# Attention softmax: ScalarE, not VectorE, multiplies the exponentials by the reciprocal sums, and TensorE asks for the weighted sample rows one step later

## What is computed

```
def cross_attend(h, k, v, w_q, w_o):
    q = einsum('btd,de->bte', h, w_q)                       # 4 heads of 256
    s = einsum('bthd,bmhd->bhtm', q, k) * 256 ** -0.5       # 256 memory rows
    p = softmax(s, axis=-1)
    o = einsum('bhtm,bmhd->bthd', p, v)
    return einsum('bte,ed->btd', o, w_o)
```

## Time and profile before

| what | value |
|---|---|
| median of 3 runs | 2838.85 us (2838.82 to 2842.92) |
| the profiled execution: its own time | 2840.13 us |
| its span, first to last instruction | 2838.4 us |
| granted TensorE clock, mean over the span | 0.939 |
| TensorE busy | 2506.3 us, 88% |
| VectorE busy | 1411.8 us, 50% |
| GpSimd busy | 1289.9 us, 45% |
| ScalarE busy | 430.7 us, 15% |

### The profile page before, as it was taken

How to read it: one execution, slowest core, us unless ns; L and a number is a source line. 1 busy time by engine, 2 the same in 40 slices (tenths; PEclk the granted TensorE clock), 3 DMA queues, 4 the chain that set the end, 5 groups by cost and what they waited for, 6 DMA issues and landing times. The chain is left out here.

```text
span 2838.4 us, 37980 instructions
## 1 busy us (share of the span) xinstructions
PE 2506.3 (88%) x14950; PEld 2403.9 (85%) x14950; DVE 1411.8 (50%) x1582; ACT 430.7 (15%) x728; POOL 1289.9 (45%) x842
## 2 busy tenths in 40 slices
PE   4967879777699689999799999999999997799996
PEld 4967879777699669888799999999999996698886
DVE  5999999999744452332622232322312234523324
ACT  3110110101111321122310000000000003211212
POOL 2734444434355454344544444444444445543452
PEclk7988999888899789999899999999999997999998
DMA  2111111111121132233011111111111111322331
GB/s 91 54 37 44 48 47 51 46 29 45 53 73 57 38 112 78 67 115 111 26 46 46 45 45 41 45 45 41 45 45 45 41 44 37 112 79 67 114 111 63
DMA packets 224013, 168.55 MB, mean 59 GB/s; under 512 B 10746, under 2 KB 219138, under 8 KB 223922
## 3 DMA queue, kind: packets, MB, share of 16 engines
q1 hardware_dynamic: 214002, 156.78, 18.0%
q10 hardware_dynamic: 9920, 10.48, 1.1%
HBM read 152.29 MB, written 14.93 MB: 59 GB/s over the span
## 5 line engine op out<-in xcount | busy, mean ns | idle before, releaser
L147 POOL TENSOR_TENSOR w_hi<-w_raw,ones 128x512 fp32r<-128x512 f32 x404 | 576.3, 1427 | 1407.4 <-PE PS L211 1225.5
L211 PE MATMUL PS<-h_hi,w_hi 128*128 128x364 f32 x2880 | 646.8, 333 | 61.0 <-DVE e_V L828 39.1
L150 POOL TENSOR_TENSOR w_lo<-w_raw,w_hi 128x512 fp32r<-128x512 f32 x404 | 644.1, 1594 | 31.7
L211 PE MATMUL PS<-h_hi,w_lo 128*128 128x364 f32 x2880 | 642.4, 332 | 0.0
L211 PE MATMUL PS<-h_lo,w_hi 128*128 128x364 f32 x2880 | 641.6, 331 | 0.0
L211 PEld LDWEIGHTS PS<-h_hi,w_hi 128*128 128x128 f32 x2880 | 502.8, 190 | 66.7 <-DVE e_V L828 40.3
L211 PEld LDWEIGHTS PS<-h_hi,w_lo 128*128 128x128 f32 x2880 | 506.6, 190 | 0.0
L211 PEld LDWEIGHTS PS<-h_lo,w_hi 128*128 128x128 f32 x2880 | 505.7, 190 | 0.0
L851 DVE SCALAR_TENSOR_TENSOR e_C<-e_V,prm,e_C 128x1024 f32<-128x1024 f32 x240 | 322.8, 1345 | 0.3
L211 PE MATMUL PS<-y_hi,w_hi 128*128 128x364 f32 x1152 | 261.6, 336 | 61.7 <-ACT e_GS L702 25.9
L211 PEld LDWEIGHTS PS<-y_hi,w_hi 128*128 128x128 f32 x1152 | 201.5, 192 | 69.5 <-issue 45.0
(11 more groups left out here) (194 smaller groups left out, 2164.0 us busy)
## 6 DMA issues: line engine op xcount, KB each, us to landing
w_raw<-in_w_in_odd SPq DMA_DIRECT2D x128, 256.0 KB, 2.8
w_raw<-in_w_in_even SPq DMA_DIRECT2D x80, 256.0 KB, 2.9
a_KV<-in_cache_mem_k SPq DMA_DIRECT2D x64, 256.0 KB, 4.9
a_KV<-in_cache_mem_v SPq DMA_DIRECT2D x64, 256.0 KB, 4.3
w_raw<-in_w_out_even SPq DMA_DIRECT2D x32, 256.0 KB, 2.7
w_raw<-in_w_k SPq DMA_DIRECT2D x32, 256.0 KB, 2.9
w_raw<-in_w_v SPq DMA_DIRECT2D x32, 256.0 KB, 2.8
w_raw<-in_w_q SPq DMA_DIRECT2D x32, 256.0 KB, 2.8
```

The lines of the kernel that those rows point to most:

```text
L147: c.nc.gpsimd.tensor_tensor(by_128(c.Wh[:, s, :]), by_128(c.Wraw[:, s % RAW, :]), ones, ALU.mult).then_inc(self.w_hi, 1)
L150: c.nc.gpsimd.tensor_tensor(c.Wl[:, s, :], c.Wraw[:, s % RAW, :], c.Wh[:, s, :].bitcast(F32), ALU.subtract).then_inc(self.w_split, 1)
L211: mm = pe.matmul(ps[:, q, 0:PART], w, a[:, q * PART:(q + 1) * PART], start=first and n == 0, stop=last and n == 2)
```

## The change

The multiplication of the prompt's `a_E` by the reciprocal of its sums moves from VectorE to ScalarE. There it is an activation `Copy` with a scale for each partition, behind `copy_turned` of the round. The two multiplications of the sample sets `a_ES` move too, to ScalarE's round 5. VectorE keeps the maxima and the reciprocals. TensorE waits for the sample sets (`s_weighed`) ahead of `turn_samples`, and no longer ahead of `turn(5)`.

```diff
@@ TensorE, round t
-                    if t == S_TURN:
-                        pe.wait_ge(s_weighed, h * SETS + SETS)
                     turn(h, t)
                     if t + 2 < NT:
                         scores(h, t + 2)
                     if t == S_TURN:
+                        pe.wait_ge(s_weighed, h * SETS + SETS)
                         turn_samples(h)
@@ ScalarE, round t
                     if t >= 1:
                         copy_turned(t - 1)
+                    act.wait_ge(inverted, h * NT + t + 1)
+                    s.activation(E[:, t % 2, :], E[:, t % 2, :], ACT.Copy, scale=SUM[:, t % 2:t % 2 + 1]).then_inc(weighed, 1)
+                    if t == S_TURN:
+                        act.wait_ge(s_inverted, h + 1)
+                        for m in range(SETS):
+                            s.activation(ES[:, m, :], ES[:, m, :], ACT.Copy, scale=SUMS[:, m:m + 1]).then_inc(s_weighed, 1)
                     if t == S_TURN + 1:
                         act.wait_ge(s_turned, h + 1)
@@ VectorE, round t
                     dve.wait_ge(exped, h * NT + t + 1)
                     v.reciprocal(SUM[:, i:i + 1], SUM[:, i:i + 1]).then_inc(inverted, 1)
-                    dve.wait_ge(inverted, h * NT + t + 1)
-                    v.tensor_scalar(E[:, i, :], E[:, i, :], SUM[:, i:i + 1], None, ALU.mult).then_inc(weighed, 1)
@@
                     if t == S_TURN - 1:
                         dve.wait_ge(s_exped, h * SETS + SETS)
                         v.reciprocal(SUMS, SUMS).then_inc(s_inverted, 1)
-                        dve.wait_ge(s_inverted, h + 1)
-                        for m in range(SETS):
-                            v.tensor_scalar(ES[:, m, :], ES[:, m, :], SUMS[:, m:m + 1], None, ALU.mult).then_inc(s_weighed, 1)
```

## The result

The changed kernel takes 2825.93 us (median of 6 runs, 2824.28 to 2831.71), the kernel before 2841.02 in its 6 runs on the same chips (2838.82 to 2844.67): 15.1 us less, a ratio of 0.995 with a 95% interval of 0.9937 to 0.9963. The profiled execution took 2825.71 us with a span of 2823.9, against 2840.13 and 2838.4.

A forecast was written before the change was run, and what follows sets the result against it. It took a ring of dependent TensorE and VectorE steps in the softmax part, filled by no engine, as the bound. -7.0 + 2.2 - 1.8 - 4.6 = -11.2 us against 2840.1 gave 2828.9, range 2824.5 to 2836.5.

The forecast's parts named there:

- VectorE is held by GpSimd's splits: Around round 5, heads 1 to 3: VectorE multiplications last until GpSimd's weight split ends, 1.23 us instead of 0.35.
- The price on ScalarE: Each moved 128x256 multiplication takes 0.51 us on ScalarE, bounds 0.47 and 0.64.
- A plain round grows by 0.20: Each ordinary softmax round: 0.51 - 0.35 + 0.04 = 0.20 us more, bounds 0.14 and 0.36.
- Turn(4) to turn(5) 2.65: Step into round 5: 2.65 us instead of 4.95 in heads 1 to 3, 3.05 in heads 0.
- Heads 1 to 3, -1.17 each: Softmax part of these six heads: 0.10 + 0.60 - 2.30 + 0.20 + 0.23 = -1.17 us each, -7.0 together.
- Heads 0, +2.2: Softmax part of the two heads 0: +0.50 through turn(6), +0.58 from turn(6) to turn(7), +2.2 us together.
- Stretched single ones -1.8: Two single stretched multiplications on the critical chain, 1.05 and 1.44 us against 0.35: -1.8 us.
- clock -4.6: TensorE's low clock between turn(5) and the values in heads 1 to 3 of layer 1 goes: -4.6 us.
- the stall moves along: Rival: GpSimd's splits hold ScalarE as they hold VectorE; slower, 2846.1 us, chance 5%.
- Dearer: Rival: ScalarE's multiplication costs more than the exponential's row; 2835.6 us at the upper bound, chance 13%.
- Hidden: Rival: values' loads or weights come late and hide the gain; 2838 to 2840 us, chance 3%.
- The clock falls all the same: Rival: low clock stays there or elsewhere in the softmax part; 2833.5 us, chance 15%.

The follow-up runs named there:

- prompt alone: Changed kernel with the 16 sample multiplications back on VectorE, ahead of round 5's reciprocal: 2838.77 us, ratio 0.9984 to the kernel before.
- order alone: Changed kernel with all multiplications back on VectorE, the samples' behind round 5's, TensorE's later wait kept: 2827.07 us, 0.9939 of the kernel before.
- out of PSUM: As order alone, but exponentials stay in PSUM and VectorE reads them from there: 2823.32 us, ratio 0.9936 to the kernel before.
- second trace of before: The kernel before, unchanged, profiled a second time: 2850.06 us, one execution.
- samples alone: Changed kernel with the prompt's 64 multiplications back on VectorE, TensorE's later wait kept: 2820.75 us, ratio 0.992 to the kernel before.

## Why the prediction was right, and where it was off

It said 2828.9 with a range of 2824.5 to 2836.5; the median is 2825.93. The signs and places of its steps held, and most of the difference of 3 us is in two sizes: what a plain round grows by, and turn(4) to turn(5).

- *VectorE is held by GpSimd's splits.* Shown: stretched pairs in "prompt alone" and "order alone", unstretched ones in "out of PSUM" at the same place. The Trainium skill ("SBUF — State Buffer", SBUF: two separate sides) has VectorE and GpSimd contend for a shared SBUF port pair; the 0.484 us from PSUM and the 2.70 us for a pair from SBUF agree.
- *The price on ScalarE.* Expected 0.51, measured 0.508, and 0.492 where one follows another, the same beside splits and without. Two in a row start 0.41 us apart, so ScalarE had 0.41 us to spare in round 6 (1152.31 in the timeline after), where the prediction had it just hidden.
- *A plain round grows by 0.20.* It grows by 0.15: the handover from VectorE to ScalarE is no dearer than the one inside VectorE was. Reciprocal to multiplication is 0.18 to 0.19 in both traces (1234.71 to 1234.90 before, 1149.70 to 1149.88 after).
- *Turn(4) to turn(5) 2.65.* 2.49 in the seven heads at full clock: besides the handover, the two reciprocals start 0.07 us apart, where I put 0.17.
- *Heads 1 to 3, -1.17 each.* At full clock turn(0) to the values went from 21.36 to 19.74, and the way to turn(0) grew by 0.12: -1.50. Six heads make -9.0 instead of -7.0, the largest error.
- *Heads 0, +2.2.* Measured is +1.7, and that it comes near is luck. In layer 1 it is 18.53 to 18.98, +0.45, less than +1.08, for the most part because the last step is 1.68 and not 1.95. Layer 0 has 19.85 to 21.07, since the low clock lasts 6.8 us there instead of 3.4. The prediction's rows on the clock leave this head out.
- *Stretched single ones -1.8, clock -4.6.* Both came as summed against the first trace: the heads of layer 1 with 23.58, 22.87 and 22.95 us are at 19.75, 19.74 and 19.74. The second trace of before shows that 4.6 was the price of one execution: there the low clock sat in four heads, for about 7.4 us. A third stretched one, of 1.00 us in layer 0 head 1, cost 0.14 us and is not in the sum.
- *Not in the sum:* the first turn(0) is 0.38 us later, and outside the softmax parts there are about 0.9 us less, mainly between them (1121.84 to 1120.49 us from the product with the values in the last head of layer 0 to turn(0) of layer 1). No cause is needed for it: between the two traces of the changed kernel the one differs by 1.0 us (1044.93 and 1043.90), the other by 3.6 (1120.49 and 1124.13).

Together -9.0 + 1.7 - 1.8 - 4.6 + 0.4 - 0.9 = -14.2, against -14.5 in the spans.

What I did not see is which half of the change pays. I forecast the whole and did not weigh its parts: the samples' move carries the gain (2820.75 alone), and the prompt's move costs some 5 us net on top of it. It adds 0.15 us in 5 rounds of 8 heads and 0.31 to the last step of heads 0, and in the traces 2.1 us of low clock in head 0 of layer 0, which "samples alone" does not have; the few held rounds that it frees are worth less.

The rivals: *the stall moves along* is out, as no multiplication on ScalarE exceeds 0.511. *Dearer* is out at 0.508. *Hidden* is out: 70.8 to 70.9 us lie between the values and the next head's turn(0) in both traces, but for the one head whose first multiplication was stretched. *The clock falls all the same* was wrong for heads 1 to 3 and right for one head 0. What makes the clock fall stays open.

## What to carry to other kernels

Before an elementwise operation is moved because its engine is busy, see whether its duration is constant: one that is now 0.35 and now 1.2 us, and ends just behind another engine's instruction, is held, and here it was enough to move those that are held on the chain. The others pay the new engine's price in every round. Reading the operand from PSUM took the hold away, too, at 0.48 us instead of 0.35. When something leaves the list ahead of a critical instruction, move the consumer's wait along with it, or the wait takes the place of what was removed.

## What had not been expected

- Two instructions in a row can be held one after the other, each by a split of its own, 2.70 us for two of 0.35. A multiplication that begins 0.16 us ahead of a split is not held ("samples alone"), but one that begins 0.02 us ahead is, for 1.44 us (2739.93 against 2739.95 in layer 1 head 3 before). Which rounds are hit hangs on tenths of a microsecond: in "samples alone" the first multiplication of a head was held in three of six heads and cost 0.8 to 0.9 us there.
- The low clock in heads 1 to 3 goes with the wait for turn(5). With 2.9 us of wait (before) 3 of 6 heads had it, in the second trace 4 of 6; with 2.17 us ("prompt alone") 1 of 6; in the other eight traces, with 1.29 us or less, none of 48. Heads 0 had it in some traces and not in others, and with equal waits: in the kernel before TensorE waits 1.57 us for turn(4) and 1.75 for turn(5) in both heads 0, and in both traces only that of layer 0 has the low clock. That the wait is the cause was not tried by itself.
